# A decoder layer on one core: which steps of a head pair carry the split of the next pair's weights

## The reference

```python
h = x @ w_in[l]
y_sb = stick_breaking_attention(sb_q, sb_k, sb_v).astype(x.dtype) @ w_sb_o[l]   # 8 heads of 64
ret = head_norm(retention(r_q, r_k, r_v)).reshape(B, S, RET_V_WIDTH)            # 4 heads
y_ret = (jax.nn.silu(r_g) * ret.astype(x.dtype)) @ w_ret_o[l]
mix = (gates[:, :, 0] * y_sb + gates[:, :, 1] * y_ret) @ w_mix_o[l]
x = layer_norm(DN_ALPHA * x + mix, ln1_g[l], ln1_b[l])
# then memory cross-attention and a SwiGLU FFN, each with its residual and layer norm
```

```python
log_rem = jnp.where(mask, jax.nn.log_sigmoid(-z), 0.0)
later = lax.cumsum(log_rem, axis=3, reverse=True) - log_rem
w = jnp.where(mask, jnp.exp(log_beta + later), 0.0)
```

## Time and profile before

| | |
|---|---|
| median of three runs | 2216.85 us (2213.17 to 2218.4) |
| the profiled execution | 2212.49 us, span 2210.5 us |
| TensorE matmul busy | 2065.8 us (93%) |
| GpSimd busy | 997.2 us (45%) |
| VectorE busy | 826.7 us (37%) |
| ScalarE busy | 521.1 us (24%) |
| mean granted TensorE clock | 0.976 of full |
| DMA | 52 GB/s over the span |

### The profile page before, as it was taken

One profiled execution on the slowest core, in us unless ns is written; L12 is line 12 of the kernel. 1 busy time (PEld: TensorE's weight loads), 2 busy tenths in 40 slices (PEclk: granted clock), 3 DMA queues, 4 the chain that ended last, 5 costly groups with the idle time before them and its releaser, 6 DMA issues.

```text
span 2210.5 us, 25755 instructions
## 1 busy us (share of the span) xinstructions
PE 2065.8 (93%) x10216; PEld 1707.3 (77%) x10216; DVE 826.7 (37%) x839; ACT 521.1 (24%) x732; POOL 997.2 (45%) x497
## 2 busy tenths in 40 slices
PE   7999999999988888998979998979999999999995
PEld 6888888788776677787858886758888888888884
DVE  5647457200265555325372325351222112112115
ACT  2413224101154444311152223151100000000013
POOL 4232232433254444445965544864444443343375
PEclk9999999999999999999989999989999999999997
DMA  5021020121100000211112110101111111111112
GB/s 185 34 71 66 28 85 29 61 79 68 39 20 20 20 24 24 106 47 48 48 58 76 57 57 29 48 29 47 47 48 47 48 47 44 51 50 53 45 42 76
DMA packets 33349, 116.34 MB, mean 53 GB/s; under 512 B 3728, under 2 KB 5136, under 8 KB 32272
## 3 DMA queue, kind: packets, MB, share of 16 engines
q1 hardware_dynamic: 27648, 93.56, 12.3%
q10 hardware_dynamic: 5648, 22.02, 2.6%
HBM read 107.18 MB, written 8.39 MB: 52 GB/s over the span
## 4 chain that ended last, share of the span: by engine, by line
PE 80%; DVE 8%; POOL 5%; issue 4%; ACT 3%; DMA 0%; POOLq 0%; DVEq 0%; ACTq 0%
PE unit L437 23%; PE unit L443 23%; PE unit L441 23%; POOL beta L387 2%; POOL w_hi L317 1%; DVE stick L1332 1%; PE aux L602 1%; PE unit L415 1%; PE aux L415 1%; PE aux L417 1%; PE aux L416 1%; PE aux L606 1%; PE unit L417 1%; PE aux L608 1%; PE unit L416 1%
## 5 line engine op out<-in xcount | busy, mean ns | idle before, releaser
L280 POOL TENSOR_TENSOR w_hi<-w_raw,one 128x1024 fp32r<-128x1024 f32 (+1 forms) x130 | 244.9, 1884 | 885.1 <-PE unit L437 885.1
L437 PE MATMUL unit<-x_lo,w_hi 128*128 128x512 f32 x1440 | 563.5, 391 | 12.8 <-POOL w_lo L294 11.2
L443 PE MATMUL unit<-x_hi,w_lo 128*128 128x512 f32 x1440 | 561.5, 390 | 0.0
L441 PE MATMUL unit<-x_hi,w_hi 128*128 128x512 f32 x1440 | 561.4, 390 | 0.0
L283 POOL TENSOR_TENSOR w_lo<-w_raw,w_hi 128x1024 fp32r<-128x1024 f32 (+1 forms) x130 | 322.1, 2478 | 10.2
L437 PEld LDWEIGHTS unit<-x_lo,w_hi 128*128 128x128 f32 x1440 | 271.0, 188 | 71.7 <-POOL w_lo L294 11.2
L443 PEld LDWEIGHTS unit<-x_hi,w_lo 128*128 128x128 f32 x1440 | 271.0, 188 | 56.8
L441 PEld LDWEIGHTS unit<-x_hi,w_hi 128*128 128x128 f32 x1440 | 271.1, 188 | 56.1
L437 PE MATMUL unit<-a_lo,w_hi 128*128 128x512 f32 x608 | 240.2, 395 | 9.8 <-DVE a_lo L1395 9.8
L443 PE MATMUL unit<-a_hi,w_lo 128*128 128x512 f32 x608 | 238.4, 392 | 0.0
L441 PE MATMUL unit<-a_hi,w_hi 128*128 128x512 f32 x608 | 236.0, 388 | 0.0
(11 more groups left out here) (258 smaller groups left out, 3260.1 us busy)
## 6 DMA issues: line engine op xcount, KB each, us to landing
w_raw<-stream SPq DMA_DIRECT2D x156, 512.0 KB, 3.2
rope_sb<-rope ACTq DMA_DIRECT2D x8, 1024.0 KB, 6.9
w_raw<-stream SPq DMA_DIRECT2D x16, 448.0 KB, 3.2
acc<-xT ACTq DMA_DIRECT2D x8, 512.0 KB, 9.6
ret_branch<-acc ACTq DMA_DIRECT2D x8, 512.0 KB, 2.6
acc<-ret_branch ACTq DMA_DIRECT2D x8, 512.0 KB, 8.0
outT<-y_out SPq DMA_DIRECT2D x16, 256.0 KB, 2.0
mem_raw<-memT ACTq DMA_DIRECT2D x1, 1024.0 KB, 5.1
```

The lines of the kernel that those rows point to most:

```text
L280: pool.tensor_tensor(w_hi[s][:, 0:width], w_raw[:, s, 0:width], one[:].to_broadcast([P, width]), ALU.mult).then_inc(w_hi_done, 1)
L437: x = pe.matmul(out, w_hi[s][:, wk], lo[:, k, cols], start=first, stop=False, skip_group_check=True)
L441: pe.matmul(out, w_hi[s][:, wk], hi[:, k, cols], start=False, stop=False, skip_group_check=True)
L443: last = pe.matmul(out, w_lo[s][:, wk], hi[:, k, cols], start=False, stop=(k == kts - 1), skip_group_check=True)
```

## The change

Only the table of the steps changes: the v chunk is split at qt 4 in place of 5, the k chunk of the next pair (in the last pair: the first chunk of the stage behind) at qt 6 in place of 7. The q chunk stays at qt 2. No instruction is added or removed.

```diff
-FILL_SPLITS = {8 * p + qt: CH_SB + 4 + 3 * p + j for p in range(SB_PAIRS) for j, qt in enumerate((2, 5, 7))}
+FILL_SPLITS = {8 * p + qt: CH_SB + 4 + 3 * p + j for p in range(SB_PAIRS) for j, qt in enumerate((2, 4, 6))}
```

## The result

The changed kernel takes 2178.57 us (median of four runs, 2177.73 to 2180.05) against 2216.14 us for the kernel before in the same rounds: a ratio of 0.9832 (95% interval 0.9815 to 0.9849), 37.6 us or 1.7% faster. The forecast was 2181 us, with a range of 2173 to 2196.

What follows compares the result with a forecast made beforehand. TensorE, busy 93% of the span, sets the time, so only its idle or half-clock time can return. Terms -11.7 - 15.1 + 1.35 - 0.75 - 10 = -36.2 us, say 36, took 2216.85 to 2181 us; range 2173 to 2196.

Steps and rivals of the forecast that it cites:

- The v chunk: Attention stage, split moved from step 5 to 4: TensorE's 2.95 us wait at step 6 goes in four pairs, 11.7 us.
- The k chunk: Split moved from step 7 to 6: TensorE's 5.02 us wait at each of three pair boundaries goes, 15.1 us.
- the rival in which the beta multiply takes the place of w_lo: Steps 4 and 6: the split delays the second head's multiply, so TensorE waits in turn_w; 2183 or 2186 us, chance 0.07.
- The rival of a mis-attributed wait: Step 6: the wait belongs to the PSUM bank, not to w_lo, and nothing moves; 2217 us, chance 0.02.
- the one that only one group pays: Boundary: something other than w_lo is as late, leaving step 6's 11.7 us and 3 us of clock; 2202 us, chance 0.05.
- What is late next: Pair boundaries: new 0.45 us wait for wT_lo, three times, 1.35 us; at the last pair's end only 0.75 of 3.12 goes.
- The clock: TensorE in the attention stage: half-clock time behind the waits returns to 2.4 GHz, 10 us gained, bounded by 0 and 10.1.
- The five stretches: TensorE at 1.2 GHz behind three boundaries and step 6 of the last two pairs, holding 20.17 us of busy time.
- a sign of being wrong: Stages after attention: a clock that falls where it did not before would show the prediction wrong; no size given.
- The rival in which the clock does not come back: Attention stage: waits go, but TensorE still falls to 1.2 GHz for as long; gain 26.2 us, 2190.7 us, chance 0.08.
- The slower rival: All 8 splits: w_hi and w_lo fall wholly onto TensorE's path, 50 us cost with half clock; 2231 us, chance 0.02.

Runs made afterwards that it cites:

- taking the collision away: Changed kernel with both split instructions of step 4 behind the second head's multiply, so no w_hi is ahead of the scan there: 2180.14 us, ratio 0.9846.
- the filler: Kernel before, with useless matmuls in TensorE's idle time ahead of the waits for the v chunk and next k chunk, no split moved: 2206.52 us, ratio 0.9960.

## Why the prediction was right

**The v chunk.** Right in the waits. The wait of step 6 went in all four pairs. Moved alone it gave 15.3 us, where the prediction's terms are 11.7 for the waits and 3 for the clock, but that this sum fits is partly luck: the trace of that run shows the waits and only 0.4 us of the clock. The w_hi of step 4 came first and held up the scan, as assumed: it lasted 1.89 us (1.9 predicted), the scan 2.92 (2.9). The second multiply and the sq_lo had room. TensorE's fill of step 5 did not wait, and taking the collision away left the time unchanged. The Trainium skill, page "SBUF — State Buffer", section "Who interferes with whom", says that the one that issues first keeps the shared ports and the other blocks, and the trace agrees with it.

**The k chunk.** Right. The multiply of step 6 ended at 719.71 and turn_w came at 721.75: 2.0 us to spare, 1.9 predicted. So the rival in which the beta multiply takes the place of w_lo did not come. Moved alone it gave 19.8 us; the prediction's terms (15.1 - 1.35 + 0.75, and about 6.7 of the 10 us of clock) make 21.2. Of the clock its trace shows 3.5. The rival of a mis-attributed wait, and the one that only one group pays, fell with these two runs.

**What is late next.** Right: wT_lo of the first head, 0.40 us three times where 0.45 was predicted, and 2.47 us at the stage's end, so that 0.65 us of the old 3.12 went where 0.75 was predicted.

**The clock.** Right in size for the whole, and the least certain step. The five stretches went, and the filler shows that they cost 9.6 us by themselves (10 predicted). What does not hold is a sharing out of this term among the waits, as in the rival in which one group pays (3 us of clock for step 6) and in what was expected of the two single moves: with either chunk moved alone, stretches grew or came at other places of the stage. In the profiled execution the sum -36.2 met 34.1 us of the stage and 32.4 us of the span. The idle time fell by 27.1 us (26.2 predicted, and the 0.9 us of line 415), the busy time by 7.0 in place of 10, because the half-clock stretch at the stage's start was twice as long and one came at its end, 3.4 us more each. Another came at 988 us, outside the stage. The prediction had named such a fall in a later stage as a sign of being wrong, but it does not come from the change: the kernel before with the filler has half clock at the same distance behind its stage (1014.4 us), and the changed kernel with both split instructions of step 4 behind the second multiply has none there. The median of before lies above its profiled run and that of after below its own, so the medians differ by 37.6. The rival in which the clock does not come back (2190.7) is refuted.

**The reason given for the clock was too simple.** The prediction said that idle times up to 1.4 us have no fall beside them. With the k chunk at step 5, two waits of 1.09 and 1.69 us with 6 us of work between had half clock behind them.

**The slower rival.** It set its point of decision at 4.5 us of lateness per moved split. The run with the w_hi done three times shows that the cost rises earlier and steeper: 3.8 us more work on GpSimd, 1.8 us beyond the room, cost 23.7 us over four splits, 5.9 us each, since the late instruction also meets a scan, and half clock follows.

## What to carry to other kernels

When a consumer waits for the last instruction of an in-order engine that is only half busy, look for the earliest point at which the buffer is free, and put the producer there: both chunks one step earlier paid 37.6 us, and the k chunk two steps earlier lost 17.4 of it, because the queue then stood in wait for the buffer. For each such move read the room of whatever is queued behind it, and then the other engine's instruction that it will start beside. Count the half clock behind waits as part of their price: here it was a quarter of the gain. But do not share it out wait by wait: with four of the seven waits gone, other half-clock stretches of the stage grew or were new, and nearly nothing came back.

## What the runs showed of the hardware

- In these traces a GpSimd tensor_tensor and VectorE's scan, both on data in SBUF, do not overlap; the one that comes first runs at its own speed and the other's duration grows by the wait. The order decides who pays: the w_hi took 1.89 us when 0.3 us ahead of the scan and 3.61 us when 0.3 us behind it; the scan of 128x1024 took 2.29 us free and 4.39 us behind a w_lo.
- That makes lateness grow: a multiply that would have been 1.8 us late for its user came 0.1 us behind a scan and was 3.8 us late.
- TensorE's clock fell to 1.2 GHz for 3.4 or 6.8 us behind waits of 2.9 to 5.0 us, not behind each of them (in the kernel before two of four equal waits of 2.9 us had none), and also behind two waits of 1.1 and 1.7 us. The length of the wait does not tell: the wait of 3.1 us at the stage's end had no half clock behind it before, and 6.8 us of it with the v chunk moved alone. Matmuls put into the seven waits kept it at 2.4 GHz there.
